# Norm and mix-split steps at other places of the recurrent loop, and the inversion's X products of levels 0 to 4 in 32x32 tiles from the third chunk on

## What is computed

```python
def rwkv7_step(state, inp):
    r_t, w_t, k_t, v_t, kk_t, a_t = inp
    sa = jnp.einsum('bhvk,bhk->bhv', state, -kk_t)
    state = (state * w_t[:, :, None, :] + sa[..., None] * (kk_t * a_t)[:, :, None, :]
             + v_t[..., None] * k_t[:, :, None, :])
    y = jnp.einsum('bhvk,bhk->bhv', state, r_t)
    return state, y
...
    mean = jnp.mean(y, axis=-1, keepdims=True)
    var = jnp.mean(jnp.square(y - mean), axis=-1, keepdims=True)
    y = (y - mean) * lax.rsqrt(var + GN_EPS)
    y = y * gn_w.reshape(RWKV_HEADS, HEAD_DIM) + gn_b.reshape(RWKV_HEADS, HEAD_DIM)
    y = y + jnp.sum(rh * kh * r_k.reshape(RWKV_HEADS, HEAD_DIM), axis=-1, keepdims=True) * vh
```

## Time and profile before

| | |
|---|---|
| runs before | 2609.5, 2610.0, 2612.53 us; median 2610.0 |
| profiled execution | 2611.29 us, span 2609.1 us |
| busy share | TensorE 98%, its weight load 79%, VectorE 59%, ScalarE 42%, GpSimd 16% |
| passes 3 to 9 | 12.6 us each |
| passes 11 to 15 | 15.5, 16.8, 16.8, 14.3, 15.4 us |

### The profile page before, as it was taken

The page is one execution under the profiler, slowest core; times in us unless marked ns, Lnnn a source line. Parts: engine busy times, 40 slices in busy tenths (PEclk is TensorE's granted clock), DMA queues, the critical chain, the costliest instruction groups (busy, mean ns, idle before and its releaser), DMA issues.

```text
span 2609.1 us, 46265 instructions
## 1 busy us (share of the span) xinstructions
PE 2544.3 (98%) x19224; PEld 2074.1 (79%) x19224; DVE 1542.4 (59%) x2343; ACT 1108.8 (42%) x1999; POOL 420.1 (16%) x368
## 2 busy tenths in 40 slices
PE   8999999999999999999999999999999999999898
PEld 6887777778778988899889777866776777798776
DVE  8765443336686665676556676365567655656753
ACT  3242233323345533655345544334444544444442
POOL 4421221100000000000000000021112100367634
PEclk9999999999999999999999999999999999999999
DMA  6743444225423453544444222631111242100032
GB/s 225 218 110 109 104 124 107 68 88 196 156 98 121 134 201 124 198 141 147 155 143 175 75 92 86 260 146 49 46 49 50 89 175 84 62 20 20 19 146 97
DMA packets 80750, 307.20 MB, mean 118 GB/s; under 512 B 7200, under 2 KB 8864, under 8 KB 62624
## 3 DMA queue, kind: packets, MB, share of 16 engines
q1 hardware_dynamic: 55984, 238.72, 26.0%
q0 software_dynamic: 12800, 33.56, 5.6%
q10 hardware_dynamic: 11760, 31.99, 3.2%
HBM read 268.32 MB, written 69.47 MB: 129 GB/s over the span
## 4 chain that ended last, share of the span: by engine, by line
PE 83%; DVE 9%; ACT 3%; issue 3%; DMA 1%; POOL 0%; DVEq 0%; ACTq 0%; SPq 0%; POOLq 0%
PE ps L428 45%; PE ps L3295 4%; PE ps L1261 4%; PE ps L1260 4%; PE ps L1262 4%; PE ps L2148 2%; PE ps L2194 2%; PE ps L2174 2%; PE ps L2075 2%; PE ps L612 2%; PE ps L638 1%; PE ps L2077 1%; PE ps L2076 1%; PE ps L627 1%; DVE parts L406 1%
## 5 line engine op out<-in xcount | busy, mean ns | idle before, releaser
L428 PE MATMUL ps<-parts,parts 128*128 128x512 f32 (+2 forms) x6456 | 1468.4, 387 | 16.7 <-DVE parts L807 9.0
L428 PEld LDWEIGHTS ps<-parts,parts 128*128 128x128 f32 x6456 | 1171.9, 188 | 300.9 <-issue 35.3
L406 DVE TENSOR_TENSOR parts<-ring,parts 128x1024 fp32r<-128x1024 f32 x180 | 220.8, 1238 | 173.4 <-ACT parts L381 168.1
L381 ACT CAST parts<-ring 128x1024 fp32r<-128x1024 f32 x195 | 201.0, 1044 | 133.1 <-DMA ring<-in_weights 66.4
L1260 PE MATMUL ps<-parts,parts 128*128 128x256 f32 x840 | 236.2, 281 | 1.3 <-ACT phase_data L1409 1.3
L1261 PE MATMUL ps<-parts,parts 128*128 128x256 f32 x840 | 236.1, 281 | 0.0
L1262 PE MATMUL ps<-parts,parts 128*128 128x256 f32 x840 | 236.0, 281 | 0.0
L406 POOL TENSOR_TENSOR parts<-ring,parts 128x1024 fp32r<-128x1024 f32 (+1 forms) x65 | 155.7, 2399 | 439.5 <-DVE parts L381 393.2
L2555 POOL TENSOR_TENSOR phase_data<-phase_data,stream 128x512 f32<-128x512 f32 x12 | 17.4, 1454 | 1186.9 <-PE ps L2085 1186.9
L870 DVE TENSOR_TENSOR_SCAN stream<-stream 128x513 f32<-128x513 f32 (+3 forms) x96 | 95.2, 992 | 173.2 <-ACT stream L740 173.0
L1260 PEld LDWEIGHTS ps<-parts,parts 128*128 128x128 f32 x840 | 158.7, 189 | 2.4 <-ACT phase_data L1409 1.5
(11 more groups left out here) (429 smaller groups left out, 3635.1 us busy)
## 6 DMA issues: line engine op xcount, KB each, us to landing
ring<-in_weights SPq DMA_DIRECT2D x128, 1024.0 KB, 4.9
up_sums<-in_weights POOLq DMA_DIRECT2D x24, 1024.0 KB, 8.8
ring<-in_weights SPq DMA_DIRECT2D x32, 512.0 KB, 4.3
ring<-up_sums SPq DMA_DIRECT2D x30, 512.0 KB, 6.0
phase_data<-up_sums SPq DMA_DIRECT2D x60, 256.0 KB, 5.7
up_sums<-up_sums POOLq DMA_DIRECT2D x8, 1024.0 KB, 5.5
phase_data<-in_weights SPq DMA_DIRECT2D x30, 256.0 KB, 5.4
raw_keep<-phase_scratch SPq DMA_DIRECT2D x21, 256.0 KB, 2.4
```

What stands on the lines that cost most here:

```text
L381: cast(self.hi(p), self.whole(p)).then_inc(self.k.hi_ready, 1)
L406: last = g.tensor_tensor(self.lo(p)[:, at], self.whole(p)[:, at], self.hi(p)[:, at].bitcast(F32), ALU.subtract)
L428: last = pe.matmul(out, a, b, start=i == 0 and a is ah and b is bh, stop=i == len(pairs) - 1 and a is al)
```

## The change

`product` gets an argument `tiled`, and `inv_x` sets it for levels 0 to 4; from chunk 2 on these products run in `blocks`: sixteen 32x32 matmuls (4 m by 4 quarters q of the partitions), each on the diagonal position of its quarter, in place of eight 64x64. The W products stay as they were. Chunks 0 and 1 still write whole 64x64 results, zeros included. Line numbers of the changed kernel are 1 lower up to line 3553 of before.

On VectorE `finish(i, 2)` moves from the end of pass i+11 to ahead of `add_t(c, 2)`, `finish(i, 3)` to pass i+12 behind `add_g(c, 1)`, two of the four `split_lo` to ahead of `add_t(15, 2)` and two into pass 16 behind `combine(14)`. On ScalarE the four `split_hi` of pass 15 move from its end to ahead of `copy_x(15, 2)`.

```diff
-        def product(c, out, lhs, rhs):
-
-            return (blocks if TILED and c >= 2 else heads)(out, lhs, rhs)
+        def product(c, out, lhs, rhs, tiled=False):
+
+            return (blocks if tiled and c >= 2 else heads)(out, lhs, rhs)
@@ inv_x
-                last = product(c, x_out(c, 0), off[:, i, 0], bc(eye))
+                last = product(c, x_out(c, 0), off[:, i, 0], bc(eye), True)
-                    last = product(c, x_out(c, l), off[:, i, l], tt[:, i])
+                    last = product(c, x_out(c, l), off[:, i, l], tt[:, i], True)
@@ ScalarE, loop of passes
             if 0 <= d < C:
                 copy_x(d, 4)
+            if c == C - 1:
+                for t in mix_tiles(0)[0:4]:
+                    split_hi(0, t)
...
-            if c == C - 1:
-                for t in mix_tiles(0)[0:4]:
-                    split_hi(0, t)
@@ VectorE, loop of passes
             if c < C:
                 open_t(c)
+            if c == C:
+                for t in mix_tiles(0)[2:4]:
+                    split_lo(0, t)
...
                 add_g(c, 1)
+            if 12 <= c < C:
+                finish(c - 12, (3,))
...
                 add_g(d, 4)
+            if 11 <= c < 15:
+                finish(c - 11, (2,))
+            if c == C - 1:
+                for t in mix_tiles(0)[0:2]:
+                    split_lo(0, t)
...
-            if 11 <= c < 15:
-                finish(c - 11, (2, 3))
-            if c == C - 1:
-                for t in mix_tiles(0)[0:4]:
-                    split_lo(0, t)
```

More of the change, by code:

```diff
@@ L2604 @@
 MASKS = LEVELS - 1
-TILED = False
 GN_EPS = 64e-5
```

## The result

The change takes **2615.64 us** (median of 20 runs, 2610.75 to 2618.54) against 2610.61 us (median of 20 runs, 2607.06 to 2614.43) for the kernel before: ratio 1.0017, 95% interval 1.0010 to 1.0024. It is slower by some 4 us by the ratio (5 by the medians), where 2600.1 us, faster by 10, was forecast; the time lies within the range. The profiled run took 2616.73 us, its span is 2614.7 us. Of the runs further down, one of the half-block kernel took 6298.96 us and is left out of its median.

What follows compares the result with a forecast made beforehand. TensorE's own work bounds passes 3 to 9; in passes 12 to 17 it idles 10.7 us, mostly awaiting VectorE. Moved steps -9.1 and tiles -0.8 sum to -9.9 us: 2600.1 us from the 2610.0 median, range 2597 to 2619.

Steps and rivals of the forecast that it cites:

- the term of the tiled X products: X products in 32x32 tiles, 5 a pass in 14 chunks: between -2.2 us and +0.6 us more, taken as -0.8 us.
- TensorE idle there: Sign that would prove the forecast wrong: TensorE idle in passes 3 to 9, or a granted clock below 1.00.
- four at a time: Four array positions run together, so a tiled product takes eight steps, 0.25 us; with waits gone 2600.1 us, chance 0.45.
- The seams: Changes of matmul shape around tiled products on TensorE: 0.12 to 0.16 us each, eating almost all the array saving.
- The saving a pass: Net gain of the five tiled products on TensorE, seams included: -0.16 us a pass, times 14 -2.2 us.
- The two at a time: Rival: only two array positions run together, sixteen steps a tiled product, +17.5 us, so 2617.6 us; chance 0.30.
- The moves: Norm and split steps moved on VectorE, ending waits of `solve` for `combine`: -9.1 us, bounds -11.0 and -4.3.
- Passes 12 and 13: Sign that the forecast holds: passes 12 and 13 at 15.5 us or less.
- The waits of 9.3 us: Five waits of TensorE's `solve` for VectorE's `combine` in passes 12 to 16: all should go, -9.3 us.
- The 1.0 us charged for steps that only come late: Moved VectorE steps delaying adds of levels 2 and 4, mostly hidden behind TensorE work: +1.0 us, bounds 0 and 5.
- the clock of pass 16: Granted clock falls behind pass 16's idle; without the long wait 0.8 us comes back, bounds 0 and 1.7.
- The rival in which the moves only move the wait: VectorE meets its next limit in passes 12 to 16 and 5 us of waits stay: 2604.9 us, chance 0.12.

Runs made afterwards that it cites:

- half-block kernel: The change with two of the four quarters left out of each tiled product, so as many instructions as before: 2595.82 us, ratio 0.9953.
- moves alone: The changed kernel with all X products as 64x64 again, only the norm and split steps moved: 2598.34 us, ratio 0.9959; measured again 2599.30 us, 0.9954.
- halves of columns: The changed kernel with X products of levels 0 to 4 as 64x64 tiles in two halves of 32 columns: 2635.68 us, ratio 1.0092.
- kernel with half of the W work: The change, with W and T products of levels 1 to 4 computing only the upper blocks from the third chunk on: 2622.19 us, ratio 1.0045.

## Why the prediction was wrong

**The step that failed** is the term of the tiled X products, -0.8 us; with the moves already in, it measured +17.3 (15 by the two ratios). Its price was counted on the array alone: steps and seams. It took for granted that the next instruction is always there, and never priced the 160 records a pass that the tiles add. The page did show the resource, in the line of the instruction queue, though its 0.4% share looks like nothing; what mattered was how long before its use each piece landed. The list of what would prove it wrong did name the sign, "TensorE idle there" in passes 3 to 9, with a granted clock below 1.00, and both came.

**The array: right.** In pass 8 of the change:

```profile
2364.47 0.45 PE L3302 MATMUL ps<-phase_scratch,stream 32*32 32x32 f32 x32
2364.75 0.48 PE L3302 MATMUL ps<-stream 32*32 32x32 f32 x32
2365.26 0.68 PE L3287 MATMUL ps<-stream 64*64 64x64 f32 x16
2365.88 0.45 PE L3302 MATMUL ps<-stream 32*32 32x32 f32 x32
2366.26 0.33 PE L3294 MATMUL ps<-phase_data,stream 64*64 64x64 f32 x4
```

The 32 records of a tiled product lie within 0.45 us (0.48 for the second of two in a row), the figure given for four at a time, and 0.28 us lies between the starts of two products in a row. The seams are 0.16 us in (2365.88 less 2365.26 + 0.68 - 0.22) and 0.12 us out (2366.26 less 2365.88 + 0.45 - 0.19), as costed from the earlier trace rows. The saving a pass is 0.11 us in the half blocks, where 0.06 was taken and 0.16 was the bound.

**The two at a time: wrong mechanism, near time.** This rival gave 2617.6 us, 2 us from what was measured, and it is refuted by the rows just shown. Without the profile after, the time alone would have confirmed it.

**The moves: right, too small.** -9.1 us was forecast, with bounds -11.0 and -4.3; measured -11.3 and, the second time, -12.3 us (by the ratios 0.9959 and 0.9954, 10.7 and 12.0, each with some 3 us to either side). Passes 13 to 17 of the moves alone:

```profile
2428.15:2443.63 15.48, 15.47 (x367) 12.72 (x367) 11.50 (x23) 7.53 (x17) 10.65 (x14) 1.00 0.01 3
2443.63:2456.05 12.42, 12.42 (x360) 11.71 (x360) 9.04 (x19) 6.20 (x14) 4.83 (x7) 1.00 0.02 4
2456.05:2468.09 12.04, 11.58 (x351) 10.90 (x345) 9.07 (x20) 5.91 (x14) 11.83 (x11) 1.00 0.25 79
2468.09:2491.59 23.50, 22.73 (x348) 18.65 (x345) 10.20 (x22) 8.06 (x17) 9.73 (x6) 1.00 0.28 96
```

Passes 12 and 13 came to 15.47 and 15.48 us here, at the 15.5 named (16.35 and 16.72 in the change, with its late pieces). The waits of 9.3 us are gone; from TensorE's 10.7 us of idle in passes 12 to 17 some 1.3 are left. The 1.0 us charged for steps that only come late was not paid: the cover named for it held. And the clock of pass 16 stays at full, which gives up to 1.7 us where 0.8 was taken. These make the -11.0 of the bound. What lies beyond it is within the uncertainty and is not assigned. The rival in which the moves only move the wait is refuted.

**What stays open.** Why a piece is asked for 0 to 1.5 us after TensorE enters the one before it in most cases, and 2 to 3.8 us in some (up to 6.3 with the W and T products tiled), has an explanation for three pieces at most (the data loads above), and that was only read off, not tried. About 1 us of the change's excess in passes 3 to 9 is not assigned. Pass 1 took 15.5 to 15.7 us in the change and in seven of the experiments, and 14.0 to 14.4 us in the kernel before and the others; the cause was not looked for. A kernel in which the tiles' records are taken out elsewhere without loss of work was not tried.

The version that beats both kernels is the moves alone: 2598.34 and 2599.30 us, 0.4 to 0.5% less than before. The tiles on levels 0 and 3 add nothing to it that was measured.

## What to carry to other kernels

A finer tiling pays on the array and costs instructions. Before splitting matmuls, count the records that TensorE runs through in each stretch and compare, for each packet of the instruction queue, when it landed with when its first record was needed. Here a lead of under 1.2 us was no lead. How dense is too dense here? An estimate from the rows of the change: a piece was asked for 1.1 us (median of passes 3 to 9) after TensorE entered the one before, was under way for 0.9 to 1.4 us, and TensorE went on 1.2 us or more after it had landed, 3.2 to 3.7 us together. In passes 3 to 15 of the kernel before no piece was run through in less than 3.5 us. Of the eight holes of over 0.6 us in those passes of the change, six stand behind a piece that was run through in 2.7 to 3.2 us, and the other two behind the data loads.

Where "issue" holes sit in the middle of a product, number the records: equal remainders mean the stream, not the program. Shifting the stream by a few harmless instructions is a cheap test of it. And a time that agrees with a rival does not show its mechanism; the rows do.

## What the runs showed of the hardware

- TensorE's instructions come in pieces of 256 records, and in these traces each piece is asked for about when TensorE enters the one before it or up to 1.5 us later, at times more. A packet takes 0.9 to 1.5 us (two of 1.7 and 2.0 us); behind a hole TensorE resumes 1.2 to 1.7 us after the packet has landed, over all kernels. One piece each 4.4 us (before) or 4.2 us (halves of columns) was supplied without a hole. With the program asking for more, the mean did not go below 3.8 us (25 in 94.0 us) and 3.9 us (31 in 120.1 us). Where the stretch is dense, records were run through far faster, a piece of 256 in 2.5 us in pass 14 of the change.
- The Trainium skill, Runtime: NRT & Kernel Launch, section "Instruction fetch mechanics", says that fetching is hidden because each instruction takes some 20 cycles to issue, slower than the fill. These runs contradict it for TensorE with small tiles: 2.5 us for 256 records is under 10 ns each, and the fetch shows at the border. What it says of 16 KB blocks and 256 instructions agrees with the packets and the remainders here.
- A hole of 1 to 2 us in TensorE's work is followed in several places by 3.4 us or more at the lower clock of 1.2 GHz (2323.5 to 2326.9 in the change, 17 us in the kernel with half of the W work), so a late piece can cost more than its hole. Behind others it is not: the hole of 2.1 us that ends at 2420.57 in the change has the full clock behind it.
- In three cases (two in the change, one with the halves of columns) the instruction packet appeared only as a data load that filled the DMA engines thinned out; that one made the other wait was not tried.
- 64x64 matmuls of 32 columns take as long as those of 64: 0.90 us for 32 records, 0.46 us for 16, each record with a weight load of its own.
